# Branch A of an attention layer: transposed scores in spans of 512 queries, with the row maximum taken off inside the product

## The reference

```python
def gqa_attend(q, k, v, mask=None, sink=None):
    s = jnp.einsum("btkgd,bskd->bkgts", q, k).astype(jnp.float32) * (q.shape[-1] ** -0.5)
    ...
        p = jax.nn.softmax(s, axis=-1)
    o = jnp.einsum("bkgts,bskd->btkgd", p.astype(v.dtype), v)

k_a, v_a = jnp.concatenate([ak, xak], axis=1), jnp.concatenate([av, xav], axis=1)
ya = sweep_query_blocks(lambda b, qb: gqa_attend(qb, k_a, v_a), aq)
    # layer 0 only, for the context tokens:
    cya = gqa_attend(caq, xak, xav)
```

## Time and profile before

| | us |
|---|---|
| median of 3 runs | 5102.31 |
| lowest, highest | 5097.14, 5107.71 |
| profiled execution | 5105.0 |
| its span | 5103.5 |
| PE busy in the span | 4590.1 (90%) |
| DVE busy | 3184.8 (62%) |
| ACT busy | 2475.0 (48%) |
| POOL busy | 1159.4 (23%) |

### The profile page before, as it was taken

One profiled execution on the slowest core, in us unless ns is written; L12 is line 12 of the kernel. 1 busy time (PEld: TensorE's weight loads), 2 busy tenths in 40 slices (PEclk: granted clock), 3 DMA queues, 4 the chain that ended last, 5 costly groups with the idle time before them and its releaser, 6 DMA issues. The chain is left out here.

```text
span 5103.5 us, 77739 instructions
## 1 busy us (share of the span) xinstructions
PE 4590.1 (90%) x27122; PEld 3796.1 (74%) x27122; DVE 3184.8 (62%) x5080; ACT 2475.0 (48%) x3061; POOL 1159.4 (23%) x857
## 2 busy tenths in 40 slices
PE   5998998888999987999985998999989987999995
PEld 2787887777878866888764887888868766787774
DVE  4762667767343557877768635677754436877776
ACT  1322555555232423777753224655633321777774
POOL 1661004410000002333334630034000001333333
PEclk8999999999999988999997999999999998999998
DMA  7645425564333566999995636332633344999998
GB/s 275 210 124 127 113 64 162 150 202 111 129 145 113 185 207 219 391 397 397 397 356 213 211 103 145 80 85 77 144 121 113 146 151 162 374 397 397 397 397 332
DMA packets 577100, 1086.97 MB, mean 213 GB/s; under 512 B 111152, under 2 KB 265008, under 8 KB 571808
## 3 DMA queue, kind: packets, MB, share of 16 engines
q1 hardware_dynamic: 530016, 932.26, 54.3%
q0 software_dynamic: 30640, 102.64, 5.4%
q10 hardware_dynamic: 16272, 49.83, 2.5%
HBM read 901.19 MB, written 183.42 MB: 213 GB/s over the span
## 5 line engine op out<-in xcount | busy, mean ns | idle before, releaser
L646 PE MATMUL project_proj_acc<-project_w_split,project_hT 128*128 128x512 f32 x2736 | 655.3, 396 | 3.4 <-DVE project_w_split L469 2.1
L1721 PE MATMUL merge_acc<-ahead_wide,merge_w_split 128*128 128x512 f32 (+1 forms) x2880 | 635.5, 375 | 19.1 <-DMA ahead_wide<-hT 11.5
L1721 PEld LDWEIGHTS merge_acc<-ahead_wide,merge_w_split 128*128 128x128 f32 x2880 | 502.9, 189 | 126.4 <-issue 18.9
L646 PEld LDWEIGHTS project_proj_acc<-project_w_split,project_hT 128*128 128x128 f32 x2736 | 510.0, 190 | 112.9 <-DVE project_hT L499 5.3
L2416 DVE TENSOR_TENSOR experts_w_gate<-experts_raw_gate,experts_w_gate 128x2048 fp32r<-128x2048 f32 x146 | 372.2, 2558 | 286.9 <-ACT experts_w_gate L2312 286.9
L2291 POOL TENSOR_TENSOR experts_w_down<-experts_raw_down,experts_w_down 128x2048 fp32r<-128x2048 f32 x73 | 351.9, 4821 | 526.2 <-ACT experts_w_down L2312 526.2
L963 DVE TENSOR_REDUCE attend_stat<-attend_scores 128x1 f32<-128x1280 f32 (+2 forms) x288 | 305.8, 1062 | 234.3 <-PE attend_scores L864 230.8
L2463 PE MATMUL experts_gate_acc<-experts_w_gate,experts_rowsT 128*128 128x512 f32 x1752 | 434.8, 404 | 12.6 <-DVE experts_rowsT L2421 8.5
L2477 PE MATMUL experts_result_acc<-experts_w_down,experts_hiddenT 128*128 128x512 f32 x1752 | 430.6, 402 | 12.2 <-DVE experts_w_down L2416 12.2
L2463 PE MATMUL experts_up_acc<-experts_w_up,experts_rowsT 128*128 128x512 f32 x1752 | 420.6, 395 | 0.0
L2463 PEld LDWEIGHTS experts_gate_acc<-experts_w_gate,experts_rowsT 128*128 128x128 f32 x1752 | 329.1, 191 | 99.6 <-issue 19.3
(11 more groups left out here) (233 smaller groups left out, 7989.8 us busy)
## 6 DMA issues: line engine op xcount, KB each, us to landing
experts_raw_gate<-in_w_exp_gate_dram SPq DMA_DIRECT2D x146, 1024.0 KB, 14.0
experts_raw_up<-in_w_exp_up_dram SPq DMA_DIRECT2D x146, 1024.0 KB, 12.8
experts_raw_down<-in_w_exp_down_dram SPq DMA_DIRECT2D x146, 1024.0 KB, 11.5
ahead_rows<-in_w_merge_dram SPq DMA_DIRECT2D x120, 768.0 KB, 6.6
attend_keys<-qk SPq DMA_DIRECT2D x128, 320.0 KB, 5.9
qk<-project_staged SPq DMA_DIRECT2D x74, 512.0 KB, 3.4
ye<-ahead_rows ACTq DMA_DIRECT2D x73, 512.0 KB, 6.3
modulation_w_ada<-in_w_ada_dram SPq DMA_DIRECT2D x24, 1024.0 KB, 26.1
```

What stands on the lines that cost most here:

```text
L646: m = pe.matmul(acc[g % 2][:, :], hT[:, a, q * KP + k, t * P:(t + 1) * P], w_split[:, n % SLOTS, c, k, :], start=(q == 0 and i == 0 and k ...
L1721: m = pe.matmul(acc[:, b, 0:w], w_split[b][:, a, k, :], hT[:, x, k, 0:w], start=(i == 0 and k == 0), stop=(i == 2 and k == KD - 1))
```

## The change

A gets a function of its own, `attend_a`, with a plan, `SpanPlan`; `attend_gqa` becomes `attend_c` and serves C alone. B is as before, except that its buffers `b_out` and `b_probsT` are also used by A.

A span is 512 queries of one head: four for each pair of heads, and in layer 0 one more for each pair, the 256 context queries of both heads. A full span has five slots, a context span one. In a slot PE makes the scores of two key tiles, transposed: keys are the weights, 512 queries stream. ACT takes the exponential straight into SBUF, where it is the streaming operand of the product with the values. Nothing is transposed back. The maximum of a query is now needed on the contraction side: the first of the two products has a 65th row, ones for the keys and the negative maximum for the queries. It comes from a product of its own, of the high parts of queries and keys with the queries as rows, in pieces of 512 columns (ten for a span: eight of one product of 512, two of two products of 256), reduced by DVE; a further product with the negated identity turns the four columns of maxima into a row, which ACT copies into the queries. Row sums come from adding the exponentials: POOL adds the first four slots, DVE the fifth and the two halves, and PE multiplies the sum by ones, in the turn-back. `SpanPlan` lays down which pieces stand behind which slot's scores (2.25 per slot, ready two slots ahead).

```diff
+class SpanPlan:
+    RATE, LEAD = 2.25, 2
...
+                        pieces += [(u + t, 1, c, [(hb, q + t, c * 512, 512, 0)]) for t in range(2) for c in range(2)]
+                        pieces.append((u, 2, 2, [(hb, q + t, NL * P, 2 * P, t * 2 * P) for t in range(2)]))
...
+                if s.n > 1 and k == min(3, len(s.pieces) - 1):
+                    self.add_row(s.n - 1)
...
+    def turn_slot(self, n):
+        if n + 1 == len(self.spans):
+            return len(self.slots)
+        if self.spans[n + 1].chunks > 1:
+            return self.last_slot(n + 1)
+        return self.spans[n + 2].first + 1
+
+    def sum_slot(self, n):
+        if self.spans[n].chunks == 1:
+            return self.last_slot(n)
+        return min(self.last_slot(n) + 3, self.turn_slot(n))
...
+def attend_a(nc, io, scr, l, nq, st, shared, rows, early):
...
+        def score(k):
+            s, c = plan.slots[k]
...
+            if k >= 2:
+                pe.wait_ge(ex.sem, ex.done(k - 2))
+            for j in range(2):
+                kt = s.tiles[2 * c + j]
+                for hb, q0, w, col in s.parts:
+                    to = tops[k % 2][:, j * 512 + col:j * 512 + col + w]
+                    pe.matmul(to, keys[v][0:HD + 1, 0, kt * P:(kt + 1) * P], high[hb][0:HD + 1, q0:q0 + w],
+                              start=True, stop=False)
+                    m = pe.matmul(to, keys[v][:, 1, kt * P:(kt + 1) * P], both[hb][:, q0:q0 + w],
+                                  start=False, stop=True)
+            m.then_inc(sc.sem, 1)
+
+        def emit_piece(p):
+            v, to = spans[p.n].pair // 2, maxes[p.index % 2]
+            if p.index >= 2:
+                old = plan.pieces[p.index - 2]
+                if old.row:
+                    pe.wait_ge(mw.sem, mw.done(old.n))
+                else:
+                    pe.wait_ge(mp.sem, mp.done(plan.reduced[old.index]))
+            if p.row:
+                pe.wait_ge(mx.sem, mx.done(p.n))
+                for t in range(4):
+                    m = pe.matmul(to[:, t * P:(t + 1) * P], row_max[:, t, :], neg_ident[:, :], start=True, stop=True)
...
+        def turn_back(n):
+            b = n % 2
+            pe.wait_ge(hc.sem, hc.done(n))
+            wait_sums(pe, n)
+            for t in range(4):
+                pe.matmul(acc[b][:, t * HD:(t + 1) * HD], halves_out[b][:, t * P:(t + 1) * P], halves[:, :],
+                          start=True, stop=True)
+            for t in range(4):
+                m = pe.matmul(acc[b][:, 4 * HD + t:4 * HD + t + 1], sums[b][:, t * P:(t + 1) * P], ones[:, :],
+                              start=True, stop=True)
...
+        def sum_values(s):
+            b, v = s.n % 2, s.pair // 2
+            if s.n >= 2:
+                pe.wait_ge(yd.sem, yd.done(s.n - 2))
...
+                    m = pe.matmul(acc[b][j * HD:(j + 1) * HD, :], values[v][:, s.tiles[2 * c + j], :], pT[:, c, j, :],
+                                  start=(c == 0), stop=(c == s.chunks - 1))
...
+        for k, (s, c) in enumerate(plan.slots):
+            score(k)
+            for p in plan.pieces_of(k):
...
+                emit_piece(p)
+            for n in range(s.n + 1):
+                if plan.turn_slot(n) == k:
+                    turn_back(n)
+            if c == s.chunks - 1:
+                sum_values(s)
...
+    def vector(dve):
...
+        for k in range(len(plan.slots)):
+            for p in plan.pieces_of(k):
+                if not p.row:
+                    reduce_piece(p)
+            for s in spans:
+                if plan.turn_slot(s.n) + 1 == k:
+                    finish(s)
+            for s in spans:
+                if plan.sum_slot(s.n) == k:
+                    add_keys(s)
...
+    def gpsimd(pool):
+        for f, n in enumerate(full):
...
+                pool.tensor_tensor(pooled[f % 2][:, :, :], pooled[f % 2][:, :, :] if c > 1 else pT[:, 0, :, :],
+                                   pT[:, c, :, :], ALU.add).then_inc(pk.sem, 1)
+            if f == 3:
+                early(pool)
...
             @block.gpsimd
             def _(pool):
+                a.gpsimd(pool)
                 b.gpsimd(pool)
-                a.gpsimd(pool)
+                if l == 0:
...
+                    with pool.Fori(NE, MAX_JOBS) as j:
+                        for c in range(0, D, 256):
+                            pool.dma_start(scr["ye"][ds(j * P, P), c:c + 256], zeros[:, :]).then_inc(cleared.sem, 16)
```

More of the change, by code:

```diff
@@ L681, in __init__ @@
         self.mask0 = (1 if t == 0 else 0) if banded and t < NL else None
-Attention = namedtuple("Attention", "sync_first scalar_first sync sync_last tensor scalar vector gpsimd qk pv yd last y_out mod")
-AttentionBuffers = namedtuple("AttentionBuffers", "const_in ident keys queries values probs probsT out stat scores acc "
-                              "halves halves_out")
-def attend_gqa(nc, io, scr, l, nq, st, shared, banded, first=None, before_it=None):
-    q_pair, k_pair, v_col, y_col = (PAIR_CQ, PAIR_CK, P, 2 * 512) if banded else (PAIR_AQ, PAIR_AK, 0, 0)
+Attention = namedtuple("Attention", "sync_first scalar_first sync sync_last tensor scalar vector gpsimd qk pv yd last y_out mod last_qk", defaults=(None,))
@@ L953, in finish @@
                 dve.wait_ge(y_out[hb].sem, y_out[hb].done(i - 1))
-            elif s % nq == 0 and first:
+            elif s % nq == 0:
                 dve.wait_ge(first.y_out[hb].sem, first.y_out[hb].done(3))
@@ L1363, in gpsimd @@
         if mod:
-            pool.wait_ge(before_it.qk.sem, before_it.qk.done(2 * nq))
-            for k in range(mod.RING):
-                mod.load(pool, 0, k)
             body(0)
```

397 lines of the change are left out of this document (320 added, 77 removed).

## The result

The changed kernel takes **5336.9 us** (median of 4 runs, 5332.5 to 5339.6), the kernel before beside it 5103.6: ratio 1.0457, 95% interval 1.0439 to 1.0476. The forecast was 5125, its range ended at 5160. The profiled execution took 5337.2 us, 232 more than the one of before, and branch A holds all of it.

What follows compares the result with a forecast made beforehand. TensorE was taken to bound A's steps; after the change, spans of 13.8 us work plus 2.2 us waiting for VectorE. Layer 1 +8.0 and layer 0 +14.3 gave +22.3 us: 5125 us, range 5062 to 5160.

Steps and rivals of the forecast that it cites:

- Side and place of the wait: Steady span of A: TensorE's maximum product after the fifth score waits 1.1 us for VectorE; slower overall at 0.48.
- the adding at 1.96 us: VectorE in each span: adding the exponentials, 128x1024 then 128x512, put at 1.225 + 0.69 + 0.05 = 1.96 us.
- Rival 3: VectorE adds while GpSimd adds: 12%, 0.25 us a span; clock falling at times, 17 a span: 5155 us; chance 0.15.
- waits of 1.1 us: TensorE behind a span's fifth score: waits 1.1 us for VectorE's maximum, making the span 16.0 us.
- Start of A: Layer 1: 9.5 us before the first score, only there at the lower clock, then span 0 at 15.0 us.
- The context spans' waits: Layer 0: 1.9 us idle before the context values and 3.5 us before a turn-back; 9.75 us per context span in all.
- The walk itself: One steady span of layer 1: 13.8 us of TensorE work plus 2.2 us of waiting, 16.0 us, 0.5 over four old steps.
- Values: TensorE in a span: 10 pairs of passes by 0.427 us, 4.4 us with the switch, where four steps took 5.0.
- turn-back passes: TensorE in a span: 16 passes, eight of them one-column, at 0.117 us each, 1.9 us against 1.04 before.
- the overhead rule: Turn-back: some 60 cycles overhead per matmul, so eight one-column passes 0.2 us, not 0.94; total some 22 us lower.
- Rival 1: TensorE runs through: VectorE's work costs less or the add finds another gap, spans near 13.8 + 0.3, 5050 us; chance 0.30.
- the 80 clearing transfers: Clearing the results with 80 DMAs instead of 20: 66 us of GpSimd beside branch C, costing nothing, 3 us as bound.

Runs made afterwards that it cites:

- e1: The changed kernel without GpSimd's three additions of a span (their sums missing from the result): 5205.4 us, ratio 1.0192.
- e7: The changed kernel with one more wait: GpSimd starts a span's additions only after VectorE has added up the span before: 5193.6 us, ratio 1.0181.
- e8: e1 with 5 extra overwritten products ahead of the product that waits behind VectorE's additions, at 26 places: 5168.4 us, ratio 1.0135.
- e4: The changed kernel with 13 extra overwritten products ahead of the maximum product that waits behind VectorE's additions, at 26 spans: 5291.8 us, ratio 1.0363.
- e5: e2 with a warmed start: extra overwritten products while TensorE waits for A's first queries and among the first maximum products: 5106.2 us, ratio 1.0011.
- e2: The changed kernel with VectorE's additions behind their own span's last scores, three score steps earlier in its queue: 5110.9 us, ratio 1.0005.
- e12: e5 with B's loads behind A's last query load, context-slot scaling before maxima, one first-step maximum product ahead of the scores: 5074.3 us, ratio 0.9943.
- e10: e5 with B's loads behind the second pair's first query load, maximum products between scores except behind row products, context-slot scaling before maxima: 5124.5 us, ratio 1.0039.
- e6: e2 with a score step's maximum products placed between its score products instead of in a row behind them: 5120.7 us, ratio 1.0043.

## Why the prediction was wrong, step by step

- **Side and place of the wait: right.** The maximum product waits for VectorE's adding in twelve of the sixteen spans of layer 1 (behind the fifth score, 3.4 to 3.7 us) and ten of the sixteen full ones of layer 0 (4.0 to 5.2 us), and slower was the likeliest side, with 0.48.
- **The step that failed: the adding at 1.96 us.** It was put together from durations of additions that ran alone. Beside GpSimd it is 4.2 (layer 1) to 4.5 us (layer 0). Rival 3 named this mechanism and put 12% on it, 0.25 us a span; it was 120 to 135%. e1 and e7 show both sides of it.
- **Where the 12% came from.** It is the ratio of two means in the earlier trace rows, 2.558 to 2.284 us. The first is a mean over 146 instructions: 16 of them started with 0.4 to 3.3 us of GpSimd's addition left and took 2.58 to 5.49 us, the rest met 0.4 us of it or none. One of the 16 in the trace of before, GpSimd's row and VectorE's:

```profile
2065.78 4.84 POOL L2291 TENSOR_TENSOR experts_w_down<-experts_raw_down,experts_w_down 128x2048 fp32r<-128x2048 f32 x1 [7.79 <-ACT experts_w_down L2312]
```

```profile
2068.15 4.62 DVE L2416 TENSOR_TENSOR experts_w_gate<-experts_raw_gate,experts_w_gate 128x2048 fp32r<-128x2048 f32 x1 [2.04 <-ACT experts_w_gate L2312]
```

  The two overlap for 2.47 us (2068.15 to 2070.62), and VectorE takes 4.62 instead of 2.28: it loses 2.34 us of 2.47. All 16 lose the overlap less 0.14 us. This is the turn-taking of the changed kernel, and by it two additions beside a GpSimd that hardly rests lose 2.6 us a span in layer 1 (0.59 and 2.02), not 0.25.
- **The step that was missing: what the wait does to the clock.** The forecast held the clock at its upper level through waits of 1.1 us, and rival 3 let it fall "at times". With 3.5 us it falls each time, and costs more than what the wait grew by: for a full span of layer 1, 16.0 us with short additions (e8), 18.6 with long ones and the clock held up (e4), 22.7 with the clock down. So 2.6 us are the contention, just what the two additions lose, and 4.1 the clock, 6.7 in all; on fourteen spans this is 94 of the 104 us that layer 1 lies above its forecast.
- **Start of A: 8.8 us a layer too low.** Span 0 was put at 15.0 and took 23.8 (3219.8 to the end of its values at 3243.6), all of its scores at the lower clock (0.43 us a product). Only the ten first products had been put at that level. e5's 21.9 against 29.8 us from the first product to the first values shows the size.
- **Layer 0.** The context spans' waits were 1.69 us (predicted 1.9) and 5.05 us before the turn-back (predicted 3.5; 3.3 without contention), each at three of four places, 1.21 and 4.8 at the last.
- **The walk itself: right in its total, in part by luck.** With short additions and the clock up a span is 15.9 to 16.0 us (predicted 16.0). But TensorE is busy for 14.6 us of it and waits 1.4 (0.55 and 0.83), where 13.8 and 2.2 were said: the products were put 0.8 us too low and the waits 0.8 too high. Values took 4.44 us at the upper clock (4.4, from 0.427 a pass; the row's 0.591 less 0.17 is 0.42), maximum and row products as said. The two kinds of turn-back passes take 8 x 2 in 1.77 us (1.9): the one-column products follow at 0.117, and the estimate of 0.2 us for all eight by the overhead rule (the Trainium skill, TensorEngine Tiling (Array Packing), Instruction Overhead) does not hold here. Scores, maxima and row products together are 8.3 us where 7.5 was said: this is where the 0.8 us lie.
- **Rival 1 was nearer than it looked**: for its 14.1 us a span it named a way, that "the add finds another gap", and e2 found one with one line (15.0 us); e12 has 14.5.
- **The rest: right.** A is 235.8 us longer and the whole span 232.0, so all else differs by 4 us; the 80 clearing transfers keep GpSimd busy for 43.3 us (predicted 66), hidden.

What is not settled: why e10's span is 15.4 us where e12's is 14.5 (no run takes its small waits apart), and which short waits bring the clock down: behind waits of 0.8 us it fell eight times of twelve in e7 and twice of eleven in e1, and behind the one of 0.55 us a span never in layer 1 of e2.

## What to carry to other kernels

Before an addition is laid beside another engine's, look for single instruction pairs in the trace that overlap, not for a mean: the mean of a group hides the few that ran together. The pairs here say what to count: what is left of the other engine's instruction at the start. Price a wait of a busy TensorE with what the clock does afterwards; here 3.5 us of idling cost 7.6 (3.5 and 4.1). And when a gain does not arrive (e5), look for the next transfer in the same queue before you doubt the gain.

## What the runs showed of the hardware

- VectorE's additions of two SBUF inputs took on average 1.95 (layer 0) and 2.46 us (layer 1) instead of 0.69 (128x512) and 2.52 and 1.74 instead of 1.22 (128x1024) while GpSimd added; GpSimd's own 2.36 rose to 2.6 and 2.8 on average. One that started beside the other engine's lost what was left of that one, less some 0.14 us. The Trainium skill names the cause (GPSIMD Engine Reference, Specifications: the SBUF interfaces are shared, with contention for VectorE instructions of two SBUF inputs), and the trace agrees; it was the size that was not expected. VectorE's maxima over 512 columns of PSUM kept 0.685 to 0.687 us in the same stretches.
- Behind every wait of 2.9 us and more in A of the changed kernel TensorE worked on at the lower clock, for 4.5 to 11 us of unbroken work at most places, and behind a wait of 1.94 us in e1 for 14 us. In layer 1 this cost 4.1 us a span beside the wait (22.7 against 18.6 in e4). Shorter waits did it at some places and not at others: of 0.8 us eight of twelve times in e7 and twice of eleven in e1 (some 1.7 us lost each time), of 1.02 us four of twelve times in e6. With these waits filled by products (e8), the spans between start and end of layer 1 kept the upper clock.
